# Gates and initial output rows worked out tile by tile in the output projection, loop reads ahead of the last wait

## What is computed

```python
y = concat([rms_norm(y_lru), rms_norm(y_swa), rms_norm(y_mem)])
h = h + y @ w_out
xt = rms_norm(h, g_ffn)
logits = xt @ w_router + b_router
top_vals, top_idx = top_k(logits, 4);  gates = softmax(top_vals)
# per expert e, over the tokens that chose it:
hh = xt @ w1[e] + b1[e]
yb = clamped_swiglu(hh) @ w2[e] + b2[e]      # x_glu*sigmoid(1.702*x_glu)*(x_lin+1)
out = h + sum over a token's 4 experts of gate * yb
```

## Time and profile before

| | us |
|---|---|
| median of 3 runs (2163.07 to 2165.44) | 2165.43 |
| profiled execution | 2162.8 |
| its span | 2161.1 |
| PE busy | 2080.2 (96%) |
| DVE busy | 1477.3 (68%) |
| ACT busy | 1192.9 (55%) |
| 16 DMA engines, hardware queue q1 | 55.9% of their time |
| seven rounds of the projection | 366.5 to 463.1 |
| first matmul of the expert loop | 503.7 |

### The profile page before, as it was taken

How to read it: one execution, slowest core, us unless ns; L and a number is a source line. 1 busy time by engine, 2 the same in 40 slices (tenths; PEclk the granted TensorE clock), 3 DMA queues, 4 the chain that set the end, 5 groups by cost and what they waited for, 6 DMA issues and landing times.

```text
span 2161.1 us, 35581 instructions
## 1 busy us (share of the span) xinstructions
PE 2080.2 (96%) x11530; PEld 1681.5 (78%) x11531; DVE 1477.3 (68%) x2291; ACT 1192.9 (55%) x1651; POOL 212.2 (10%) x201
## 2 busy tenths in 40 slices
PE   6999989988999999999999999999999999999997
PEld 4443678866799778877979797977779979888895
DVE  3251486668866787688676767678986666567666
ACT  3241375246645676567564646477764555555545
POOL 2000300012101111011010101011010110101001
PEclk9999999989999999999999999999999999999999
DMA  7000302118966699689686868679996677668556
GB/s 269 1 0 6 144 27 88 40 55 321 357 227 207 231 340 355 194 324 358 232 275 240 268 234 262 231 258 368 336 373 212 194 242 273 185 206 297 188 197 219
DMA packets 203128, 477.39 MB, mean 221 GB/s; under 512 B 14743, under 2 KB 20951, under 8 KB 203024
## 3 DMA queue, kind: packets, MB, share of 16 engines
q1 hardware_dynamic: 185598, 437.69, 55.9%
q0 software_dynamic: 17424, 39.17, 7.5%
q10 hardware_dynamic: 66, 0.02, 0.0%
HBM read 468.99 MB, written 32.11 MB: 232 GB/s over the span
## 4 chain that ended last, share of the span: by engine, by line
PE 71%; DVE 10%; issue 7%; DMA 6%; ACT 4%; DVEq 1%; ACTq 1%; POOLq 1%; SPq 0%; POOL 0%
PE ps L1288 16%; PE ps L1290 16%; PE ps L1289 16%; PE ps L1023 8%; DVE w_lo L1842 4%; DMA out<-y,idx_cur 4%; PE ps L1401 2%; DMA ring<-in_w 1%; PE ps L1168 1%; PE ps L1170 1%; PE ps L1169 1%; PE ps L1282 1%; ACT ring L719 1%; DMA xh<-in_x 1%; DVE xT L1842 1%
## 5 line engine op out<-in xcount | busy, mean ns | idle before, releaser
L890 ACT ACTIVATE w_hi<-ring 128x1024 fp32r<-128x1024 f32 x730 | 781.7, 1121 | 422.1 <-PE ps L1290 370.0
L1842 DVE TENSOR_TENSOR w_lo<-ring,w_hi 128x1024 fp32r<-128x1024 f32 x732 | 862.3, 1220 | 188.3 <-ACT w_hi L890 188.3
L1288 PE MATMUL ps<-xT,w_hi 128*128 128x256 f32 x1248 | 354.2, 284 | 0.0
L1290 PE MATMUL ps<-xT,w_lo 128*128 128x256 f32 x1248 | 353.1, 283 | 0.0
L1289 PE MATMUL ps<-xT,w_hi 128*128 128x256 f32 x1248 | 353.1, 283 | 0.0
L1288 PE MATMUL ps<-w_hi,xT 128*128 128x512 f32 x816 | 323.3, 396 | 13.2 <-issue 6.9
L1289 PE MATMUL ps<-w_lo,xT 128*128 128x512 f32 x816 | 319.5, 392 | 0.0
L1290 PE MATMUL ps<-w_hi,xT 128*128 128x512 f32 x816 | 319.5, 391 | 0.0
L1288 PE MATMUL ps<-w_hi,actT 128*128 128x512 f32 x644 | 262.8, 408 | 0.0
L1290 PE MATMUL ps<-w_hi,actT 128*128 128x512 f32 x644 | 251.6, 391 | 0.0
L1289 PE MATMUL ps<-w_lo,actT 128*128 128x512 f32 x644 | 251.1, 390 | 0.0
(11 more groups left out here) (312 smaller groups left out, 2400.7 us busy)
## 6 DMA issues: line engine op xcount, KB each, us to landing
ring<-in_w SPq DMA_DIRECT2D x390, 1024.0 KB, 7.2
xh<-in_x SPq DMA_DIRECT2D x4, 2048.0 KB, 16.1
work<-in_w_out SPq DMA_DIRECT2D x1, 4096.0 KB, 12.9
token_rows<-uT POOLq DMA_DIRECT2D x8, 512.0 KB, 2.9
out<-xh SPq DMA_DIRECT2D x8, 512.0 KB, 9.1
work<-in_w_in SPq DMA_DIRECT2D x2, 1536.0 KB, 18.0
uT<-in_w_mem_kv SPq DMA_DIRECT2D x1, 2048.0 KB, 14.5
ring<-in_w_in SPq DMA_DIRECT2D x1, 1536.0 KB, 16.9
```

Source lines behind the costliest of these rows:

```text
L890: act_e.activation(hi, raw, ACT.Copy).then_inc(hi_ready, counted(h, whole))
L1288: pe.matmul(acc, hi, whi, start=first, stop=False, skip_group_check=shared)
L1290: return pe.matmul(acc, lo, whi, start=False, stop=last, skip_group_check=shared)
L1842: return dve.tensor_tensor(lo, x, hi.bitcast(F32), ALU.subtract)
```

## The change

The exponentials, gates, their words and transposes, and the products with b2 are made tile by tile in the rounds, two to four rounds behind: in round i ACT takes the exponentials of tile i-2 and loads the Exp and the Sqrt table, DVE makes gates and low words of tile i-2, PE turns the gates of tile i-3 and multiplies the halves of tiles i-3 and i-4, and DVE adds them (`init_rows`). PE's `init_row` is gone, and all 16 half rows are DVE's. The router product stands behind the last chunk of its round. A wait is added ahead of `turn_row(i)` for the initial rows of tile i-3 (tile 3 at the most), since both use bank 6. Tiles 4 to 7 follow after the rounds. The b2 words are made in the attention (ACT in items 6, 8 and 11, DVE in item 12). The b1 rows are cleared by POOL in round 6, and their words are made in round 7 by ACT and DVE. SP stores the first four tiles earlier. PE's wait for the initial rows stands inside the loop's body, behind its reads; SP's stands ahead of the loads of slots 4 and 5. The b1 matmul stands three k steps later. The two groups of a gather signal two semaphores. The memory places of some tiles move. The hunks on memory, and some of the removals, are left out below.

```diff
-            sp.wait_ge(op_done, 6 * NT)
-            for k in range(3):
-                sp.dma_start(b2_sb[k * E:(k + 1) * E, :], b2[0]).then_inc(b2_in, 16)
+            def store_rows(t):
+                sp.wait_ge(init_d, 2 * t + 2)
+                sp.dma_start(out[0, t * P:(t + 1) * P, :], xh[:, t, :]).then_inc(init_out, 16)
+
+            store_rows(0)
+            store_rows(1)
             sp.wait_ge(b1_zero, 1)
             for half in range(2):
                 sp.dma_start(b1_raw[half * E:(half + 1) * E, :], b1[0]).then_inc(b1_in, 16)
+            store_rows(2)
+            store_rows(3)
             sp.wait_ge(ttab_ready, 1)
+            sp.wait_ge(init_d, 2 * NT)
...
-            for i in range(NT):
-                if i < NA:
-                    sp.wait_ge(init_a, i + 1)
-                sp.wait_ge(init_d, i + 1 if i < NA else 2 * i + 2 - NA)
...
             for i in range(NT):
                 po.wait_ge(xr_ready, i + 1)
                 po.dma_start(xrows[i * P:(i + 1) * P, 0:D], xrow[i % 2]).then_inc(xrow_out[i % 2], 16)
+                if i == NT - 3:
+                    po.wait_ge(out_lo_ready, word_at[NT - 1, 0])
+                    po.memset(b1_raw, 0.0).then_inc(b1_zero, 1)
...
+                if j == 6:
+                    act_e.wait_ge(b2_in, 48)
+                    act_e.wait_ge(ylru, LT)
+                    act_e.activation(b2_top, b2_raw[2 * E:3 * E, :], ACT.Copy).then_inc(b2_hi, 1)
+                elif j == 8:
+                    act_e.activation(b2_r[0:2 * E, :], b2_raw[0:2 * E, :], ACT.Copy).then_inc(b2_hi, 1)
+                elif j == 11:
+                    for a, n in ((b2_r[3 * E:P, :].rearrange("p (a b) -> p a b", b=P), KD), (gatesT_r[3 * E:P, :, :], 2)):
+                        act_e.activation(a, ident[3 * E:P, :].rearrange("p (a b) -> p a b", a=1).to_broadcast([E, n, P]),
+                                         ACT.Copy, scale=0.0).then_inc(b2_hi, 1)
                 if j == 4:
                     act_e.wait_ge(wout_in, 32)
                 elif j == 7:
...
+            def exponentials(t):
+                act_e.wait_ge(ex_in, t + 1)
+                act_e.activation(ex[:, t, :], ex[:, t, :], ACT.Exp).then_inc(ex_done, 1)
+
+            def gate_hi(ts):
+                act_e.wait_ge(gates_ready, min(ts[0], last_gates) + 1)
+                if ts[0] >= 2:
+                    act_e.wait_ge(gt_done, ts[0] - 1)
+                a = ts[0] % 2
+                for k in (0, 2):
...
+                if i >= 2:
+                    exponentials(i - 2)
+                    act_e.preload_act_table(ACT.Sqrt)
                 if i + 1 < NT:
                     row_hi(i + 1, 0)
+                if i >= 3:
+                    take_gates((i - 3,))
+                if i + 1 < NT:
+                    row_hi(i + 1, 1)
+                if i == NT - 1:
+                    act_e.wait_ge(b1_plus, 1)
+                    act_e.activation(b1w[:, :].rearrange("p (j two c) -> p j two c", j=4, two=2),
+                                     b1_raw.rearrange("p (j c two) -> p j two c", j=4, two=2), ACT.Copy).then_inc(b1_hi, 1)
                 if i:
                     take_turned(i - 1)
+                if i >= 2:
+                    gate_hi((i - 2,))
                 if i + 1 < NT:
-                    row_hi(i + 1, 1)
                     row_hi(i + 1, 2)
                 act_e.wait_ge(op_out, 6 * i + 6)
-                if i:
-                    act_e.wait_ge(h_sq, i)
-                act_e.activation(sqtmp[:, 0, :], xh[:, i, :], ACT.Square, accum_out=st[:, i:i + 1]).then_inc(h_sq, 1)
+                if i >= 2:
+                    act_e.wait_ge(lg_done, i - 1)
+                act_e.activation(uT[:, 9 + i % 2, :], xh[:, i, :], ACT.Square, accum_out=st[:, i:i + 1]).then_inc(h_sq, 1)
...
+            def init_product(t, half):
+                if half == 0:
+                    pe.wait_ge(gt_out, t + 1)
+                    pe.wait_ge(b2_hi, 4)
+                    pe.wait_ge(b2_lo, 1)
+                bank, n = init_bank(t, half), 2 * t + half
+                if bank == 6:
+                    pe.wait_ge(xt_out, 2 * t + 6)
+                    if n:
+                        pe.wait_ge(init_d, n)
+                elif t < last_gates:
+                    pe.wait_ge(op_out, 6 * (NT - 1) + bank + 1)
+                elif t == NT - 1:
+                    pe.wait_ge(init_d, n - 3)
+                pe.matmul(ps[:, bank, :], gatesT_r[:, t % 2, :], b2_r[:, half * HALF:(half + 1) * HALF],
+                          start=True, stop=True).then_inc(init_mm, 1)
+
+            def turn_gates(t, bank, at):
+                pe.wait_ge(g_lo, min(t, last_gates) + 1)
+                if t < NT - 3:
+                    pe.wait_ge(lg_out, t + 2)
+                elif t == NT - 3:
+                    pe.wait_ge(op_out, 6 * NT)
+                pe.transpose(ps[0:3 * E, bank, at * P:(at + 1) * P],
+                             gates3[:, t % 2, :, :].rearrange("p k e -> p (k e)"), ident[:, :]).then_inc(gt_done, 1)
 
             def turn_row(i, m2):
                 if m2 == 0:
                     pe.wait_ge(xr_ready, i + 1)
                 if 2 * i + m2:
                     pe.wait_ge(xt_out, 2 * i + m2)
+                if i >= 3 and m2 == 0:
+                    pe.wait_ge(init_d, 2 * min(i - 2, NT - 4))
...
             for i in range(1, NT):
                 for n in range(6):
                     chunk(i, n)
-                    if n in (2, 3):
-                        turn_row(i - 1, n - 2)
-                    elif n == 4:
+                    if n == 1 and i >= 4:
+                        init_product(i - 4, 1)
+                    elif n in (3, 4):
+                        turn_row(i - 1, n - 3)
+                    elif n == 2 and i >= 3:
+                        turn_gates(i - 3, 7, 0)
+                    elif n == 5:
+                        if i >= 3:
+                            pe.wait_ge(gt_out, i - 2)
                         route_logits(i - 1)
-            pe.wait_ge(op_out, 6 * NT)
-            init_row(0)
+                        if 3 <= i < NT - 1:
+                            init_product(i - 3, 0)
+            for half in range(2):
+                init_product(NT - 4, half)
+            turn_gates(NT - 3, 5, 0)
             for m2 in range(2):
                 turn_row(NT - 1, m2)
...
-            for kind, i in init_units[:EARLY_A + 1]:
-                init_product(kind, i)
+            for at in range(2):
+                turn_gates(last_gates + at, 7, at)
+            for t in (last_gates, NT - 1):
...
 
-            pe.wait_ge(xg_in, 32)
+            pe.wait_ge(xg_in[0], 16)
...
-            pe.wait_ge(init_d, 2 * NT - NA)
+            pe.wait_ge(b1_taken, 1)
...
                             if j == 0:
                                 pe.wait_ge(xlo_ready[g], nth[g] + 1)
                         acc = ps[:, 2 * (j % 2) + g, :]
-                        if kh == 1:
-                            if j == 0:
-                                pe.wait_ge(b1_lo, 1)
-                                pe.wait_ge(sel_ready, p + 1)
-                            pe.matmul(acc, sel[:, :], b1w[:, j * HALF:(j + 1) * HALF], start=False, stop=False)
                         for k in range(4):
+                            if kh == 1 and k == 3:
+                                if j == 0:
+                                    pe.wait_ge(b1_lo, 1)
+                                    pe.wait_ge(sel_ready, p + 1)
...
 
+                    pe.wait_ge(init_d, 2 * NT)
                     up(0, 0)
                     pe.wait_ge(idx_ready, p + 1)
                     if len(groups) == 2:
                         for g in groups:
                             pe.wait_ge(combined[g], halves[g] + 1)
+                        pe.wait_ge(xg_in[1], p16 + 16)
                         transpose_x(1, 6)
...
                     softmax_in(j + 2)
+                if j == 12:
+                    dve.wait_ge(b2_hi, 2)
+                    dve.tensor_tensor(b2_r[2 * E:3 * E, :], b2_raw[2 * E:3 * E, :], b2_top.bitcast(F32), ALU.subtract).then_inc(b2_lo, 1)
                 if j - 1 in word_step:
...
+            def gates_of(a, b):
+                dve.wait_ge(ex_done, b)
+                gs, ts, n = gates[:, a:b, :], slice(a, b), b - a
+                link(dve.tensor_tensor(gs, ex[:, ts, :], mask[:, ts, :], ALU.mult))
+                link(dve.tensor_reduce(st[:, 32 + a:32 + b], gs, AX_X, ALU.add))
+                link(dve.reciprocal(st[:, 40 + a:40 + b], st[:, 32 + a:32 + b]))
+                dve.tensor_tensor(gs, gs, st[:, 40 + a:40 + b].rearrange("p (t a) -> p t a", a=1).to_broadcast([P, n, E]),
+                                  ALU.mult).then_inc(gates_ready, 1)
+
+            def gate_lo(a, b):
+                dve.wait_ge(g_hi, 2 * min(a, last_gates) + 2)
+                s, n = a % 2, b - a
+                dve.tensor_tensor(gates3_r[:, s:s + n, 1, :], gates[:, a:b, :], gates3[:, s:s + n, 0, :],
```

(75 more changed lines are left out.)

169 lines of the change are left out of this document (65 added, 104 removed).

## The result

The changed kernel takes 2171.11 us (median; 2169.83 for the profiled execution, span 2168.1) against 2165.43 before. The ratio is 1.0030, with a 95% interval of 1.0022 to 1.0039: slower by 0.3%, where the prediction said 0.2% faster. The median is above the top of the predicted range, 2168. One of its nine executions took 4885 us, for a reason that no trace here shows, and is not in the ratio.

A forecast was written before the change was run, and what follows sets the result against it. PE was taken to bound rounds and loop, dependent steps the stretch between: +1.0+2.4+3.1-1.1-9.8-0.3 = -4.7 us, median 2160.7 against 2165.4. The forecast's own range was 2157.5 to 2163.5, the 8-in-10 range 2155.5 to 2168.

The forecast's parts named there:

- The bound: Projection rounds bound by PE; from 463 us, dependent steps from last chunk to the loop's first matmul at 503.68.
- Attention: Attention items 6, 8, 11, 12: b2 words mostly hidden, 1.0 us left in item 11; +1.0, bounds 0 and 4.8.
- Rounds 3 to 6: Projection rounds: PE's added transposes and products, 0.4 then 0.6 each, plus 0.2 for mode changes; +2.4 us.
- ties: Rounds 4 to 6: DVE's half row meets PE at `turn_row`, ACT's row_hi meets DVE; no wait, no reserve.
- Rival 2: Rounds 4 to 7: late ACT chain makes DVE, then PE wait at `turn_row`; +6.3, 2171.7 us; chance 0.12.
- Round 7: Last projection round: PE waits 4.3 us at `turn_row` behind the b1 words; +3.1 us, bounds 0 and 5.5.
- rival 3: Before the loop: 0.5 to 1.5 us per round or PE at half clock after its wait; -1, 2164.4; chance 0.18.
- From the last chunk to the last mask: After the rounds: PE's first `init_row` pair goes, norm and choice stay; 12.5 us become 11.4, -1.1.
- From the mask to the loop: Last mask to first matmul: earlier table chain, first matmul at +18.0 instead of +27.8; -9.8 us, bounds -7.5 and -11.
- what hides beneath: Mask to loop: last half rows, low words and turn of x, POOL's low words covered; cover thin, 1 to 2 us.
- The loop: Loop passes: later place saves most of PE's 0.9 us wait for `sel`; -0.3 us, bounds -0.9 and +3.
- the four: Rivals: no round 7 wait (0.15), late ACT chain (0.12), half that or half clock (0.18), late loop weights (0.07).

The follow-up runs named there:

- both edits: Changed kernel with POOL waiting for the table before its low words and b1's low words moved behind tile 4's initial half rows: 2153.73 us, ratio 0.9963.

## Why the prediction was wrong, point by point

**The bound** was read rightly: the dependent steps from the last chunk to the loop's first matmul, and the rounds, decide. Nearly everything that moved the time is there.

**Attention**: +0.8 against +1.0. Right. The two fills in item 11 took 1.05 and 0.40.

**Rounds 3 to 6**: +2.2 against +2.4. Right, ties included: PE waits for nothing in rounds 4 to 6. Rival 2, the slower one, fails with it, and gets no share in the slowdown. The timeline of ACT after, in round 6:

```profile
442.72 0.23 ACT L817 ACTIVATE ring<-ring 128x32 f32<-128x32 f32 x1 [1.46 <-DVE ring L1809]
442.97 1.28 ACT L838 ACT_TABLE_LOAD   x1
444.26 0.53 ACT L752 ACTIVATE lru_words<-uT 128x384 fp32r<-128x384 f32 x1
```

The words follow 0.01 us behind the load, so the drain of 1.38 us that the Trainium skill (ScalarE: Activation LUTs, What ACT_TABLE_LOAD costs) adds to each load is not paid here.

**Round 7**: +4.4 against +3.1 (the prediction's own steps add up to 16.8, not 16.9). The wait was 4.0 us, the forecast 4.3. The term was too small by PE's half clock behind it: the granted clock was 0.61 from 466 to 470.4, against 1.00 over the same matmuls, 462 to 466, with the words of b1 late. The text had this in the upper bound, 5.5, and in rival 3, and took the value without it.

**From the last chunk to the last mask**: +0.3 against -1.1. The initial rows did leave, but work in their place was what kept PE's clock up: the router product behind them took 3.62 instead of 1.87, 1.75 more, which is over the whole miss of 1.4. Useless products in their place brought it back to 1.97. It isn't the gap of round 7 that does it: with the words of b1 late, PE has no gap there, and the product takes 3.62 all the same. The clause of the working that failed is the one by which norm and choice "stay": the router product between them did not.

**From the mask to the loop**: -2.7 against -9.8. This is the step that failed, and in it one clause: under "what hides beneath" the text put "POOL's first two low words by +14", as a transfer of work to an idle engine that needs only to be in time. It counted when POOL's results come, not what POOL's work does to DVE in the same stretch. Moving `limit` and the low words ahead of the wait for the table put 9.46 us of POOL onto the only 4 us in which DVE's small operations on SBUF are the whole chain, and that cost 9.84 (10.08 less 0.24). The rest went better than forecast: without the block the table would have been ready 11.8 after the mask's end instead of 13.0, and the first matmul came 3.5 after the table, not 5.0. So 9.8 - 1.2 - 1.5 = 7.1, the whole miss. With POOL's wait put back, this stretch lasted 15.5 us (482.64 to 498.18) instead of 28.1, better than the foretold 28.1 - 9.8 = 18.3.

Rows that should have warned were in the trace of before. One was among those read: the 3.28 us of b1's low words, which the prediction itself noted as taken "with POOL at work beside" and priced at 2.4 without. It drew the right number for the operation that it moved away from POOL, and not the question of which operations now stand beside POOL. The subtraction of 2.32 us (L1735) and the cast of 0.83 were not read at all.

**The loop**: +0.3 against -0.3. PE's wait for `sel` did go, but from the first matmul to the end the fourteen profiled executions lie between 1653.9 and 1661.6, so neither value can be told.

**The rivals.** None of the four was it. That POOL and DVE get in each other's way had no chance at all, so the range, which ended at 2168, had no room for it. Rival 3's mechanism, the half clock, was there, as about 3 us on top.

## What to carry to other kernels

Before work is moved to POOL or to another time on POOL, list what DVE runs in that stretch, of which kind it is and where its operands are. Here operations that read PSUM went on beside POOL at full speed. Beside POOL's subtractions TENSOR_SCALAR and TENSOR_TENSOR on SBUF alone stood still, the small ones too; beside its fills TENSOR_SCALAR and CAST did, but not operations with two inputs in SBUF. A busy engine is then no sign of work: look for an instruction whose time is far above its neighbours' of the same size, and for another engine's row that ends at the same moment. And PE's clock is part of every edit: a wait of 4.0 us cost 5 with the slower matmuls behind it, and products taken away from a stretch in which PE otherwise waits saved nothing, since the step behind them ran at half clock.

## What the runs showed of the hardware that was not expected

- One small operation of DVE (32 columns, 0.24 us) was held for 10.08 us over four instructions of POOL, and for 5.39 over two. The hold must have begun before POOL's recorded time: the operation should have ended at 493.30, and POOL's row begins at 493.64. POOL's second gather issue, from 492.61 to 493.62, isn't the reason: with both edits the same operation ran 0.44 us into the same issue (487.38 and 487.82) and took 0.24. But half-precision one-hots, started while POOL was already at work, got in at POOL's ends, about one for each, and so did large float32 low words, so the number format doesn't decide it. Why the one is held over all and the others are not stays open.
- The hold goes both ways: with two large operations of DVE on SBUF beside them, POOL's four took 11.49 us instead of 9.54.
- PE's first read of the table from SBUF, 1.12 us in the kernel before, took 0.49 in the kernel after, and those of the first pass 0.30. In the kernel before the stores of the initial rows were under way at that time; the DMA share from 497 to 500 was 1.01. After, it was 0.00 from 507 to 509. The rows of PE's queue, before and then after:

```profile
L1300 PEldq TENSOR_LOAD <-ttab x1: 1123/1123/1123, 498.8 to 498.8; - x1
```

```profile
L1338 PEldq TENSOR_LOAD <-ttab x1: 492/492/492, 507.0 to 507.0; - x1
L1340 PEldq TENSOR_LOAD <-ttab x32: 302/308/324, 508.1 to 2113.1; - x32
```

Loads alone are not enough: in all 32 passes of the loop after, with a mean DMA share of 0.76, no read of this line took over 0.33. That the stores slow the reads was not tried by itself.
